# State space decays on ScalarE and VectorE, gate quarters spread over four chunks, group norms by quadrant sums between output panels

## What is computed

```python
def step(state, inp):
    xc, ac, bc, cc = inp
    acum = jnp.cumsum(ac, axis=1)
    seg = jnp.where(causal, acum[:, :, None] - acum[:, None, :], -jnp.inf)
    scores = jnp.einsum('btgn,bsgn->btsg', cc, bc)[..., None] * jnp.exp(seg)
    y_diag = jnp.einsum('btsgh,bsghp->btghp', scores, xc)
    y_off = jnp.einsum('btgn,bghpn->btghp', cc, state) * jnp.exp(acum)[..., None]
    w_end = jnp.exp(acum[:, -1:] - acum)
    new_state = (state * jnp.exp(acum[:, -1])[..., None, None]
                 + jnp.einsum('bsgn,bsghp->bghpn', bc, xc * w_end[..., None]))
    return new_state, y_diag + y_off
...
y = y + d_skip.astype(jnp.float32)[:, None] * xs.astype(jnp.float32)
y = y.reshape(b, s, M_D_INNER) * jax.nn.silu(z.astype(jnp.float32))
yg = y.reshape(b, s, M_GROUPS, M_D_INNER // M_GROUPS)
yg = yg * lax.rsqrt(jnp.mean(yg * yg, axis=-1, keepdims=True) + EPS)
y = yg.reshape(b, s, M_D_INNER) * norm_g.astype(jnp.float32)
return y.astype(h.dtype) @ out_w
```

## Time and profile before

| | us |
|---|---|
| median of 3 runs (lowest to highest) | 1510.21 (1508.72 to 1511.82) |
| the profiled execution, its own time | 1510.82 |
| its span in the profile | 1509.0 |
| PE busy, whole span | 1391.1 (92%) |
| DVE / ACT / POOL busy | 858.8 / 554.8 / 466.3 |
| state space, four chunks, 874.5 to 1086.1 | 211.7 |
| output panels 0 to 6 and seven eighths of the last, 1086.1 to 1171.1 | 85.0 |

### The profile page before, as it was taken

One profiled execution on the slowest core, in us unless ns is written; L12 is line 12 of the kernel. 1 busy time (PEld: TensorE's weight loads), 2 busy tenths in 40 slices (PEclk: granted clock), 3 DMA queues, 4 the chain that ended last, 5 costly groups with the idle time before them and its releaser, 6 DMA issues. The chain is left out here.

```text
span 1509.0 us, 19330 instructions
## 1 busy us (share of the span) xinstructions
PE 1391.1 (92%) x7776; PEld 1092.8 (72%) x7776; DVE 858.8 (57%) x997; ACT 554.8 (37%) x720; POOL 466.3 (31%) x223
## 2 busy tenths in 40 slices
PE   5998889889999998999999879986899899999997
PEld 3777666658888886887788757664587689777775
DVE  3789663476555653325757556777863651455553
ACT  4323546233222222113444424444532332455541
POOL 0000000039988877997000023332100050132220
PEclk9999889979999999998899989997899899999999
DMA  9332042205455444552322332423222342111121
GB/s 387 131 140 112 29 171 109 84 29 204 185 192 193 171 172 171 190 219 84 115 84 87 108 96 67 133 65 99 75 84 84 117 163 85 56 57 57 56 84 56
DMA packets 41350, 181.10 MB, mean 120 GB/s; under 512 B 3393, under 2 KB 20161, under 8 KB 21313
## 3 DMA queue, kind: packets, MB, share of 16 engines
q1 hardware_dynamic: 41280, 180.12, 33.1%
HBM read 173.75 MB, written 6.36 MB: 119 GB/s over the span
## 5 line engine op out<-in xcount | busy, mean ns | idle before, releaser
L193 DVE TENSOR_TENSOR wlo<-raw,whi 128x2048 fp32r<-128x2048 f32 x95 | 253.7, 2670 | 193.8 <-ACT whi L189 190.9
L271 PE MATMUL ps<-hhi,whi 128*128 128x512 f32 x640 | 252.0, 394 | 2.4 <-PEq L562 0.8
L271 PE MATMUL ps<-hhi,wlo 128*128 128x512 f32 x640 | 249.4, 390 | 0.0
L271 PE MATMUL ps<-hlo,whi 128*128 128x512 f32 x640 | 249.1, 389 | 0.0
L189 ACT ACTIVATE whi<-raw 128x2048 fp32r<-128x2048 f32 x95 | 181.5, 1911 | 150.6 <-PE ps L1312 96.3
L200 POOL TENSOR_TENSOR ada_raw<-ada_raw,cs 128x2048 f32<-128x2048 f32 x36 | 146.6, 4073 | 206.8 <-DVE h2lo L451 148.1
L209 POOL TENSOR_TENSOR ada_raw<-ada_raw 128x1024 f32<-128x1024 f32 x72 | 164.1, 2280 | 5.6
L1785 POOL TENSOR_TENSOR dec<-dec,cb 128x512 f32<-128x512 f32 x32 | 60.9, 1903 | 297.4 <-ACT dec L1751 297.4
L271 PEld LDWEIGHTS ps<-hhi,whi 128*128 128x128 f32 x640 | 120.2, 188 | 28.6 <-issue 2.4
L271 PEld LDWEIGHTS ps<-hhi,wlo 128*128 128x128 f32 x640 | 120.1, 188 | 25.8
L271 PEld LDWEIGHTS ps<-hlo,whi 128*128 128x128 f32 x640 | 120.3, 188 | 24.4
(11 more groups left out here) (372 smaller groups left out, 2887.6 us busy)
## 6 DMA issues: line engine op xcount, KB each, us to landing
raw<-panels SPq DMA_DIRECT2D x95, 1024.0 KB, 4.9
ada_raw<-ada SPq DMA_DIRECT2D x48, 1024.0 KB, 6.8
first<-ada SPq DMA_DIRECT2D x8, 1024.0 KB, 20.7
bc<-ac_rows SPq DMA_DIRECT2D x32, 256.0 KB, 4.5
x_kept<-x SPq DMA_DIRECT2D x2, 2048.0 KB, 9.7
x<-x_kept SPq DMA_DIRECT2D x2, 2048.0 KB, 8.8
x<-x_in SPq DMA_DIRECT2D x1, 2048.0 KB, 9.3
out<-y SPq DMA_DIRECT2D x8, 256.0 KB, 2.2
```

The lines of the kernel that those rows point to most:

```text
L193: e.tensor_tensor(wlo[:, c % 2, :, :], raw[:, c % 2, :, :], whi[:, c % 2, :, :].bitcast(F32), ALU.subtract).then_inc(lo_split, 1)
L271: mm = e.matmul(ps[:, 2 * (qc % 2) + b, :], w[:, c % 2, 2 * k + b, :], src[part][:, k, :], **flags)
```

## The change

- `dec` of batch n is now made by ScalarE with four Relus of 128x128, relu(a_s - a_t), one for each head with its column of `acc_c` as bias, and an exp with scale -1. VectorE, not GpSimd, multiplies by `cb`, in `masked(n)`. GpSimd has no work here. VectorE's difference and clip are gone.
- `bc`, `dec` and `ce` have three buffers instead of two (`seg_t` is gone). SP may load bc(n) when decays(n-3) has read its buffer.
- Each chunk lays out with four z quarters (before: 4, 4, 4, 0), and 5, 4, 3 and 4 lie ahead of batches (before: 7, 7, 6, 0). `taken_at` follows: panels 0 to 7 are taken behind batches 0, 6, 8, 14, 16, 23, 24 and 31.
- The decay of the state moves behind each group's skip.
- Square sums are made as four matmuls with 32 columns of ones, one for each quadrant of positions, so that root and reciprocal are 128x128 instead of 128x512; `group_spread` brings the result to all partitions with four small matmuls, and the norm reads it from PSUM.
- `squares` of groups 0 and 1 lie behind batches 28 and 30, those of 2 and 3 and three of the spreads between the matmuls of the first three output panels. Low parts follow each norm.

```diff
-            IN_LAYING = [4, 4, 4, 0]
-            IN_BATCHES = [7, 7, 6, 0]
+            IN_LAYING = 4
+            IN_BATCHES = [(1, 2, 4, 5, 7), (1, 3, 5, 7), (1, 4, 6), (1, 2, 4, 6)]
             LAYING_OUT, QUARTERS = [], []
+            k = 0
             for c in range(TB):
-                k = sum(IN_LAYING[:c]) + sum(IN_BATCHES[:c])
-                LAYING_OUT.append(range(k, k + IN_LAYING[c]))
+                LAYING_OUT.append(range(k, k + IN_LAYING))
+                k += IN_LAYING
                 for b in range(NB):
-                    j = k + IN_LAYING[c] + b - (NB - IN_BATCHES[c])
-                    QUARTERS.append(range(j, j + 1) if b >= NB - IN_BATCHES[c] else range(0))
+                    n = int(b in IN_BATCHES[c])
+                    QUARTERS.append(range(k, k + n))
...
-                bc = sbuf(tmp, "bc", [P, 2, HB, P])
-                seg_t = sbuf(tmp, "seg_t", [P, 2, HB, P])
-                dec = sbuf(tmp, "dec", [P, 2, HB, P])
-                ce = sbuf(tmp, "ce", [P, 2, HB, P])
+                bc = sbuf(tmp, "bc", [P, 3, HB, P])
+                dec = sbuf(tmp, "dec", [P, 3, HB, P])
+                ce = sbuf(tmp, "ce", [P, 3, HB, P])
...
                             c, b = n // NB, n % NB
-                            if n >= 2:
-                                sp.wait_ge(M["clip"], n - 1)
-                                if n - 2 >= NB:
-                                    sp.wait_ge(M["grow"], n - 1 - NB)
-                            sp.dma_start(bc[:, n % 2, :, :],
+                            if n >= 3:
+                                sp.wait_ge(M["seg"], n - 2)
+                                if n - 3 >= NB:
+                                    sp.wait_ge(M["grow"], n - 2 - NB)
+                            sp.dma_start(bc[:, n % 3, :, :],
                                          ac_rows[b * HB:(b + 1) * HB, c * P:(c + 1) * P].unsqueeze(0)
-                                         .to_broadcast([P, HB, P])).then_inc(M[f"bc{n % 2}"], 16)
+                                         .to_broadcast([P, HB, P])).then_inc(M[f"bc{n % 3}"], 16)
                             for p in taken_at(n - 2) if n >= 2 else ():
                                 load_panel(sp, c0 + p + 4, 0)
 
...
-                                          stop=t % 4 == 3).then_inc(G["ss"], 1)
+                                for b in range(TB):
+                                    mm = pe.matmul(ps[32 * b:32 * b + 32, 4 + g % 2, 0:P], ones[:, 0:32],
+                                                   gsq[:, t % 4, b * P:(b + 1) * P], start=t % 4 == 0, stop=t % 4 == 3,
+                                                   skip_group_check=True)
+                                mm.then_inc(G["ss"], 1)
+
+                        def group_spread(g):
+                            pe.wait_ge(G["rs"], g + 1)
+                            for b in range(TB):
+                                mm = pe.matmul(ps[:, 4 + g % 2, b * P:(b + 1) * P],
+                                               ident[:, 32 * b:32 * b + 1].to_broadcast([P, P]), state[:, g, 0:P],
+                                               start=True, stop=True)
+                            mm.then_inc(G["spread"], 1)
 
...
+                                    if c == TB - 1:
+                                        if 2 * g + b == 4:
+                                            squares(0)
+                                        if 2 * g + b == 6:
+                                            group_spread(0)
+                                            squares(1)
...
-                                parts = hi_lo(4 * g + j)
+                                if (k, j) == (0, 1):
+                                    group_spread(1)
+                                if (k, j) == (0, 3):
+                                    squares(2)
+                                if (k, j) == (1, 1):
+                                    group_spread(2)
+                                if (k, j) == (1, 2):
+                                    squares(3)
+                                if (k, j) == (2, 0):
+                                    group_spread(3)
...
+                        def decays(n):
+                            c, b = n // NB, n % NB
+                            act.wait_ge(M[f"bc{n % 3}"], 16 * (n // 3 + 1))
+                            if n >= 3:
+                                act.wait_ge(M["yd"], n - 2)
+                            for j in range(HB):
+                                h = b * HB + j
+                                one = act.activation(dec[:, n % 3, j, :], bc[:, n % 3, j, :], ACT.Relu,
+                                                     bias=acc_c[:, c, h:h + 1], scale=-1.0)
+                            one.then_inc(M["seg"], 1)
+                            if c:
+                                act.activation(ce[:, n % 3, :, :], bc[:, n % 3, :, :], ACT.Exp).then_inc(M["grow"], 1)
+                            act.wait_ge(M["seg"], n + 1)
+                            act.activation(dec[:, n % 3, :, :], dec[:, n % 3, :, :], ACT.Exp,
+                                           scale=-1.0).then_inc(M["dec"], 1)
+
+                        turned = 0
...
+                            for b in range(NB):
+                                n = c * NB + b
+                                decays(n)
+                                if b == 1 and c < TB - 1:
+                                    act.wait_ge(M["bt"], 6 * c + 5)
+                                    if c:
+                                        act.wait_ge(M["st"], MG * c)
+                                    act.activation(btok[:], ps[:, 4, :].rearrange("p (g t) -> p g t", g=MG),
+                                                   ACT.Copy).then_inc(M["btok"], 1)
+                                if c == TB - 1 and b == 3:
+                                    group_squares(0)
+                                if c == TB - 1 and b == 6:
+                                    group_squares(1)
+                                for p in taken_at(n) if n < NN - 2 else ():
                                     take_z(p)
...
                         group_std(0)
+                        for n in (NN - 2, NN - 1):
+                            for p in taken_at(n):
+                                take_z(p)
                         group_std(1)
-                        group_squares(MG - 1)
                         hi_part(act, 0)
+                        for p in range(turned, MT // 2):
+                            silu_z(p)
+                        group_squares(2)
+                        hi_part(act, 1)
                         group_std(2)
-                        hi_part(act, 1)
...
+                        def masked(n):
                             c, b = n // NB, n % NB
-                            dve.wait_ge(M[f"bc{n % 2}"], 16 * (n // 2 + 1))
-                            if n >= 2:
-                                dve.wait_ge(M["dec"], n - 1)
-                            dve.tensor_tensor(seg_t[:, n % 2, :, :], bc[:, n % 2, :, :],
-                                              acc_c[:, c, b * HB:(b + 1) * HB].unsqueeze(2).to_broadcast([P, HB, P]),
-                                              ALU.subtract).then_inc(M["seg"], 1)
-                            dve.wait_ge(M["seg"], n + 1)
-
-                            dve.tensor_scalar(seg_t[:, n % 2, :, :], seg_t[:, n % 2, :, :], 0.0, None,
-                                              ALU.min).then_inc(M["clip"], 1)
+                            dve.wait_ge(M["dec"], n + 1)
+                            if b == 0:
+                                dve.wait_ge(M["cbm"], c + 1)
+                            dve.tensor_tensor(dec[:, n % 3, :, :], dec[:, n % 3, :, :],
+                                              cb[:, b // 2, :].unsqueeze(1).to_broadcast([P, HB, P]),
+                                              ALU.mult).then_inc(M["mat"], 1)
                             if c:
...
                                               ALU.mult).then_inc(M["cbm"], 1)
-                            difference(c * NB)
+                            masked(c * NB)
+                            masked(c * NB + 1)
...
-                                    if n % NB < NB - 1:
-                                        difference(n + 1)
+                                    if g < MG - 1:
+                                        masked(n + 2)
                                     for p in taken_at(n):
                                         split_lo(dve, c0 + p + 2, 0)
+                                if c == TB - 1 and g == MG - 1:
+                                    norm_lo(dve, 0)
+                                    group_rs(dve, 1)
                                 dve.wait_ge(M["yd"], 2 * gi + 2)
...
+                                if 0 < c < TB - 1:
+                                    s3 = state[:, g, :].rearrange("p (h d) -> p h d", h=GH)
```

(19 more changed lines are left out.)

97 lines of the change are left out of this document (33 added, 64 removed).

## The result

| kernel | median, us | range of the runs | ratio to before, 95% interval |
|---|---|---|---|
| before | 1509.5 | 1507.4 to 1511.8, 4 runs | |
| changed | 1540.7 | 1539.2 to 1541.7, 4 runs | 1.0206 [1.0187, 1.0225] |

What follows compares the result with a forecast made beforehand. The section was taken as bound by TensorE's work plus a chain through SP's weight load that delays bc. Chunks 13.1, panels 6.5 and clock 9.1 sum to 28.7 us more: 1539.0 us, range 1500 to 1556.

Steps and rivals of the forecast that it cites:

- waits ahead of batches 3, 11, 19, 27: TensorE stalls before each chunk's fourth batch, because bc lands late: 9.4, 7.6, 10.6 and 8.7 us.
- third state matmul, chunk 1: At chunk 1's end, VectorE's split_lo lies ahead of the last skip, so TensorE waits 3.5 us more.
- load behind split_lo, bc behind load: In SP's queue, the weight load goes only at split_lo's end, with the next bc issued 0.4 us later.
- the clock's 1.3 us pieces: Work behind long TensorE waits runs at low clock: 1.3 us each, counted seven times, 9.1 us in all.
- four chunks together: State space section: 224.8 us against 211.7 before, 13.1 us more, with the clock's loss counted separately.
- panels and what follows, over before: Output panels: spreads, square sums and a first wait add 6.5 us; the clock's loss at the first panel is separate.
- The walk: Following the section's new program order link by link with earlier prices; chunk 1 comes to 54.7 us against 54.05.
- U: End of the laying out's third quarter, 12.56 us into chunk 1; in chunk 3 the fourth quarter, 14.8 us in.
- Rival (a): Weight load does not hold the broadcasts, so the four long waits go: faster, about 1498 us; chance 0.18.
- Rival (b): Same chain but shorter, bc in 4.5 us, Relus at 0.25 us, no clock loss: 1520 us; chance 0.16.
- rival (c): No change: the shorter chain, plus chunk 3's Squares hidden under its four quarters: 1510 us; chance 0.06.
- Rival (d): ScalarE becomes the bound, Relu near 0.5 us each, 16 us dearer: 1555 us; chance 0.08.
- The rule: Skill page's advice to use VectorE for relu; at its 0.41 us per Relu the sum would be some 5 us higher.

Runs made afterwards that it cites:

- the second experiment: The kernel before with each weight load on SP moved three bc issues later and nothing else: 1505.8 us, ratio 0.9982.
- the single Relu: The changed kernel with one 128x512 Relu for four 128x128 ones per batch, three heads' decays left wrong: 1536.0 us, ratio 1.0177.
- the tuned kernel: The changed kernel with weight loads three bc issues later, and laying-out take_z, last split_lo of chunks 0 to 2, and chunk 3's Squares and sums later: 1470.3 us.

## Why the prediction was right, point by point

| step | predicted | measured in the changed kernel |
|---|---|---|
| waits ahead of batches 3, 11, 19, 27, us | 9.4, 7.6, 10.6, 8.7 | 9.40, 7.97, 10.59, 7.17 |
| third state matmul, chunk 1 | 3.5 | 2.95 (chunk 2: 3.61) |
| load behind split_lo, bc behind load | at once, 0.4 | 0.03, 0.45 |
| chunks 0 to 3, the clock's 1.3 us pieces in | 57.3, 57.3, 54.4, 63.6 | 57.9, 58.9, 55.2, 66.0 |
| four chunks together | 232.6 | 237.9 |
| panels and what follows, over before | +7.8, clock in | +5.9 |
| start of the section | no term | -1.3 |
| whole | +28.7 | +30.9 (span) |

**The walk held.** In chunk 1 the prediction has take_z and split_hi end at U + 2.75, decays(9) at 5.0, masked(9) at 6.3, split_lo and the load at 11.9, bc(11) read at 17.9, TensorE released at 21.4. The rows above give 2.9 (946.57), 5.2, 6.5 for the first three, 12.1 and 12.2 for split_lo's end and the load, 18.3 and 22.1. Every link came 0.1 to 0.7 us late and none was missing. The mechanism is the one that the prediction names, and the load three issues later bears it out. The sign rested on one reading: SP's load goes 0.1 us behind split_lo's end. In the old kernel the same load cost only 3 us (the second experiment), so its price could not be read off the old waits; only the walk in the new order gave it.

**Rival (a)** was the reverse of that reading, and the load three issues later gives its price: 1504.5 against the 1498 that the rival names, with bc issued ahead of the load. **Rival (b)** asked for bc in 4.5 us (measured 5.7 from issue to read in chunk 1), Relus at 0.25 us (measured pitch 0.29) and no loss by the clock: none came, and rival (c), which builds on (b), fell with it. **Rival (d)** fell with the single Relu.

**Terms mis-sized.** The four chunks took 5.3 us more than forecast. Behind them the forecast was 1.9 us too high, and the section began 1.3 us earlier, for which the sum has no term; so the whole is nearer than its parts, by luck.

In chunk 3 the walk behind U held. ScalarE's take_z started at 1062.04, which is U; batch 27 ran at U + 20.4, batch 28 at U + 29.4 and the first output panel at U + 49.1, against 20.1, 29 and 48.8. The waits there were shorter than the walk has them (7.17 us ahead of batch 27, not 8.7; 3.50 ahead of batch 28, not 4.8) because TensorE came to them later, and the slow quarter behind batch 27 (3.64 us instead of 2.99) was hidden in the next wait. What made the chunk 2.4 us longer is U itself, 16.9 us in instead of 14.8. The first quarter, behind the state wait of 3.61 us, took 4.57 us at a granted clock of 0.67 (columns as above):

```profile
1045.16:1049.73 4.57, 4.57 (x15) 3.25 (x14) 0.69 (x2) 0.00 (x0) 0.00 (x0) 0.67 0.01 4
```

The sum has 1.3 us for it, in the table's row of chunk 2. The quarters behind the long waits of chunks 0 to 2 took 4.95, 4.22 and 3.63 us: 12.8 together, where three at 4.29 make 12.9, so this price was right on average. What the sum leaves out is the batches right behind the waits: batch 19 took 1.92 us (1024.40 to 1026.32) and batch 27 1.93, where 1.07 was counted. How much of this reached the end of each chunk, and how much a later wait hid, is not worked out. In busy time the clock took more: TensorE runs the same matmuls of the four chunks in 151.0 us in the tuned kernel and in 170.7 in the changed one, at granted clocks of 0.96 to 1.00 and 0.82 to 0.89.

Behind the chunks, the panels took 6.4 us more than before (91.36 against 85.00), and 6.5 were forecast. The first quarter of the first panel took 3.01 us (1111.14 to 1114.15), behind a wait of only 0.98, so the 1.3 us for the clock did not fall due there; the rest of the span was 0.5 us shorter than before.

**Costed inside the sum, not apart.** The prediction walks the new order as a whole. It names the fourth chunk's 63.6 against 53.5 but not that the spreading as such costs 15 us while chunks 0 to 2 wait. Three of my later expectations (quarters with the load later, load later in the old kernel, take_z later) failed on the same point: a chunk's time was taken as a sum of work and known waits, when a wait that is removed uncovers the next one.

**The rule weighed.** The changed kernel's Relus average 389 ns (the price taken from the earlier trace rows was 394). Four in a row take 1.17 us to the next instruction, so they overlap by 0.1 us each. The Trainium skill (page "ScalarE: Activation LUTs", section "Rules for kernel authors") prices one at about 0.41 us, an estimate that the row bears out for one and that overstates four by 0.5 us. What its advice to keep relu off ScalarE would be worth here, no run shows: the one-Relu kernel, 4.8 us faster, still has a Relu there. The table loads of the changed kernel take 1283 ns with 0.0 to 0.1 us of idle ahead of those in the batches, as before; the 2.66 us that the page gives with a drain does not show.

## What to carry to other kernels

Before work is moved between engines, write down for each DMA queue what stands behind an issue that waits: a small transfer queued behind a load whose buffer an engine frees late inherits that engine's whole chain, and the trace then blames the last multiply. Here one line in SP's queue was worth 3 us in the old order and 35 in the new. And judge a spreading of filler work only after the waits are gone: the same distribution cost 12 to 15 us while chunks waited and gave 7 once they did not.
